# Rotary angles computed on 32 columns and spread through DRAM instead of on 512 columns in place

## Chip, cores and metric

One core of a Trainium2 chip runs the whole kernel. The metric is the device time of one execution in microseconds (us).

## What is computed

A two-layer decoder trunk on 512 tokens of width 1024: in each layer a token mixer (windowed attention with rotary positions, a gated delta rule, a causal convolution module) and a channel mixer. All matrix products are made of three products of split fp32 parts. What matters here is the rotary part: 8 frequencies, 512 positions, and the first 16 of every 64 head rows rotated.

```python
inv_freq = ROPE_THETA ** (-jnp.arange(0, ROT_DIM, 2, dtype=jnp.float32) / ROT_DIM)   # 8 values
ang = positions.astype(jnp.float32)[..., None] * inv_freq                              # 512 x 8
cos = jnp.cos(ang)[:, :, None, :]
sin = jnp.sin(ang)[:, :, None, :]
...
r1 = (x1 * cos - x2 * sin).astype(x.dtype)
r2 = (x2 * cos + x1 * sin).astype(x.dtype)
return jnp.concatenate([r1, r2, x[..., ROT_DIM:]], axis=-1)
```

## The kernel before

Activations lie feature-major: a tile holds 128 features on the partitions and 512 tokens as columns. Every engine has its own program, written out by hand, and the engines meet through semaphores; each engine does its instructions in order. A weight tile is loaded (`load_tile`, SyncE), its high part is written by ScalarE (`split`, L1293), the rest by VectorE (`split`, L1766), and TensorE makes 24 matmuls of 512 columns from it (`part`, L660). Two raw buffers alternate, so SyncE loads tile g when VectorE has split tile g - 2.

*Start.* SyncE issues, one after another, the parameters (L453), the positions broadcast to 128 partitions (L454), the last 9 columns of the constants (L455), the first constants (L456), x (L457), eight conditioning tiles of 1 MB (`load_ada`, L419), weight tiles 0 and 1 and the remaining constants. TensorE turns each conditioning tile into a row (L623), ScalarE copies it (L1347), TensorE sums it into columns (L631). When all eight are done, VectorE forms the modulation and `sclg`. ScalarE has split weight tiles 0 and 1 by then. Then, for each of 8 chunks k, ScalarE writes `hhi` (L1319), and VectorE the full value (L1861) and `hlo` (through the helper at L1756). TensorE bridges the wait with filler matmuls (`busy`, L687) and then does `first_pair` (L674 to L676): 48 matmuls, the two first weight tiles against the chunks as they come, and behind it the gates (L708 to L710).

*Angles.* On GpSimd, right behind a fill of `ZERO`: cast the positions, multiply by the frequency of the partition, then a range reduction for sine and cosine, 13 operations each (L561 to L571), with a semaphore wait behind every one (`turn`). All are on `ang`, 128x512, although only 32 of 128 rows carry an angle. ScalarE takes the sines in its step t = 2 (L1495, L1496), into `sinb` and `cosb`. VectorE masks the rows that are not rotated in its step t = 10 (L2046, L2047). Its `roped` (L1967) uses both five times in each layer, from step t = 13 on.

*Shared memory.* `posi` and `ang` lie in the room of conditioning tiles 8 and 9. So `load_ada(8)`, which SyncE comes to in its step t = 3 between weight tiles 5 and 6, waits on semaphore `sincos` (L414). Behind it on SyncE's list stand tile 9, weight tile 6 and a block of zeros for the DRAM array `xs`.

*Steps around it.* In step t = 4 ScalarE splits weight tile 6; at t = 5 it loads the table of logarithms and writes the logarithm of the key norms (`rows_logged`, L1389), then splits tile 7. TensorE uses that logarithm in `combine_rows` (L725, L726), behind tile 5 and ahead of tile 6.

Of the kernel before, what the change touches and what calls it, by code (L numbers as in the profile page):

```python
# [11 lines left out]
F32 = mybir.dt.float32  # L12
F32R = mybir.dt.float32r
I32 = mybir.dt.int32
# [4 lines left out]
P = 128  # L19
# [25 lines left out]
for _n, _w in (("ident", 128), ("ones", 128), ("pick", 1), ("eps", 1), ("pick8", 8), ("bones", 128), ("rot", 128), ("istk", 64), ("amask", 256),  # L45
               ("lev", 6 * 64), ("reset", 512), ("rows", 512), ("spread", 8 * 64), ("selg", 256),
               ("heads", 4 * 8), ("comb_r", 8), ("comb_l", 8), ("col_r", 16), ("col_l", 16), ("col_g", 16),
               ("i32", 32), ("half", 2), ("sign", 1), ("qscale", 1), ("rotm", 1), ("nrotm", 1), ("before", 128), ("blocks", 16), ("rank", 8), ("invf", 1)):
    C_COLS[_n] = (_at, _at + _w)
    _at += _w  # L50
N_CONST = _at
# [39 lines left out]
ORDER = [DK, DK + 1, DQ, DQ + 1, DV, DV + 1, CB, CB + 1, CA, CA + 1, V0, K0, Q0, Q0 + 1, Q0 + 2, Q0 + 3, DZ, DZ + 1]  # L91
I_CB, I_CA, I_V, I_K, I_Q, I_DZ = 6, 8, 10, 11, 12, 16
I_INV = 9


BY_PE = tuple(range(G_IN)) + (G_GATE, G_FFN - 1)
# [8 lines left out]
def constants():  # L105
    c = np.zeros((P, N_CONST), np.float32)

    def put(name, a):
        lo, hi = C_COLS[name]
        c[:a.shape[0], lo:hi] = a.reshape(a.shape[0], hi - lo)  # L110
# [58 lines left out]
    put("sign", np.where(p < 4, -1.0, 1.0)[:, None])  # L169
    put("qscale", np.where(p < 4, 0.0, -0.5 * np.log(64.0))[:, None])  # L170
    inv = np.float32(500000.0) ** (-np.arange(0, ROT, 2, dtype=np.float32) / np.float32(ROT))
    d = p % 64
    put("invf", np.where(d < ROT, inv[d % (ROT // 2)], 0.0)[:, None])
    put("rotm", (d < ROT)[:, None] * 1.0)
    put("nrotm", (d >= ROT)[:, None] * 1.0)
    put("eps", np.full((P, 1), EPS))
    put("rank", np.tile(8.0 - np.arange(8), (P, 1)))
    put("before", (p[:, None] < p[None, :]) * 1.0)
# [5 lines left out]
def trunk(nc, xT, consts, params, pos, ada, w8, w11, wm, outT):  # L184
    ctx = ExitStack()
    with ctx:
        def sb(name, shape, dt=F32, stack=ctx):
            return stack.enter_context(nc.sbuf_tensor(name, [P] + shape, dt))
# [3 lines left out]
        def sem(name):  # L192

            if name not in sems:
                sems[name] = ctx.enter_context(nc.semaphore(name))
            return sems[name]
# [24 lines left out]
            cact = sb("cact", [DC], stack=room)  # L221
        with ExitStack() as room:
            sb("below", [6 * KD * P + 13 * 1024], stack=room)
            posi = sb("posi", [S], I32, stack=room)
            ang = sb("ang", [5, S], stack=room)
        with ExitStack() as room:
            sb("above", [6 * KD * P + 25 * 1024 + 512], stack=room)
            wbah = sb("wbah", [DC * 8], F32R, stack=room)
# [28 lines left out]
            grow = sb("grow", [D], stack=room)  # L257
        xs = nc.dram_tensor("xs", (NB * P, D), F32, kind="Internal").ap()
        ys = nc.dram_tensor("ys", (NB * P, D), F32, kind="Internal").ap()

        def rawm_tile(g):
            return rawm[:, g % RING, :]
# [146 lines left out]
        def _(sp):  # L409

            def load_ada(g):

                if g == G_IN:
                    sp.wait_ge(sem("sincos"), 2)  # L414
                if g == G_GATE + 2:
                    sp.wait_ge(sem("ada_used"), G_GATE + 1)
                elif g >= G_IN + 2:
                    sp.wait_ge(sem("ada_acc"), summed(g - 2))
                sp.dma_start(adar(g), ada[g, :, :]).then_inc(sem(f"landed{ada_ring(g)}"), 16)  # L419
# [31 lines left out]
                sp.dma_start(out, src).then_inc(sem(f"tile_in{g % 2}"), 16)  # L451

            sp.dma_start(par[:], params).then_inc(sem("par_in"), 16)  # L453
            sp.dma_start(posi[:], pos.partition_broadcast(P)).then_inc(sem("pos_in"), 16)  # L454
            sp.dma_start(cst[:, N_CONST - 9:], consts[:, N_CONST - 9:]).then_inc(sem("pos_in"), 16)  # L455
            sp.dma_start(cst[:, 0:N_FIRST], consts[:, 0:N_FIRST]).then_inc(sem("cst_in"), 16)  # L456
            sp.dma_start(x[:], xT.rearrange("(c p) s -> p c s", p=P)).then_inc(sem("x_in"), 16)  # L457
# [5 lines left out]
            for t in range(N_IN_TILES):  # L463
                load_tile(t + 2)
                if t == 0:
                    sp.wait_ge(sem("zeroed"), 1)
                if t < NB:
                    sp.dma_start(xs[t * P:(t + 1) * P, :], ZERO).then_inc(sem("xs_cleared"), 16)
                if t == 3:
                    load_ada(G_IN)  # L470
                    load_ada(G_IN + 1)
                if t == 6:
                    load_ada(G_IN + 2)
                    load_ada(G_IN + 3)
# [62 lines left out]
        def _(pool):  # L537

            for name in ("bank_free0", "bank_free1", "glo_ready"):
                pool.sem_inc(sem(name), 1)  # L540
            pool.memset(ZERO, 0.0).then_inc(sem("zeroed"), 1)

            two_pi = 2 * np.pi
            c1 = 6.28125
            c2 = float(np.float32(np.round((two_pi - c1) * 2 ** 17) / 2 ** 17))
# [5 lines left out]
            def turn(ins):  # L551

                turned[0] += 1
                ins.then_inc(sem("ang_step"), 1)
                pool.wait_ge(sem("ang_step"), turned[0])

            pool.wait_ge(sem("pos_in"), 32)
            turn(pool.tensor_copy(ang[:, 0, :], posi[:]))
            turn(pool.tensor_scalar(ang[:, 0, :], ang[:, 0, :], C("invf"), None, ALU.mult))
            for n, shift in ((2, 0.0), (3, 0.25)):  # L560
                turn(pool.tensor_scalar(ang[:, 1, :], ang[:, 0, :], float(1 / two_pi), shift, ALU.mult, ALU.add))  # L561
                turn(pool.tensor_scalar(ang[:, 1, :], ang[:, 1, :], magic, None, ALU.add))
                turn(pool.tensor_scalar(ang[:, 1, :], ang[:, 1, :], magic, None, ALU.subtract))
                prev = ang[:, 0, :]
                for cc in (c1, c2, c3, c4):
                    turn(pool.tensor_scalar(ang[:, 4, :], ang[:, 1, :], -cc, None, ALU.mult))
                    turn(pool.tensor_tensor(ang[:, n, :], ang[:, 4, :], prev, ALU.add))
                    prev = ang[:, n, :]
                turn(pool.tensor_scalar(ang[:, n, :], ang[:, n, :], float(two_pi * shift), float(np.float32(3.1415925)),
                                        ALU.add, ALU.min))  # L570
                turn(pool.tensor_scalar(ang[:, n, :], ang[:, n, :], -float(np.float32(3.1415925)), None, ALU.max))  # L571

            pool.wait_ge(sem("xs_cleared"), 16 * NB)
            pool.wait_ge(sem("slots_ready"), 1)
# [702 lines left out]
        def _(act):  # L1277
# [86 lines left out]
            for layer in range(DEPTH):  # L1364
# [103 lines left out]
                for t in range(I_FILL):  # L1468
# [21 lines left out]
                    if t == 2:  # L1490
                        soft_plus()
                        gates()
                        if layer == 0:
                            act.wait_ge(sem("ang_step"), 2 + 2 * 13)
                            act.activation(sinb[:], ang[:, 2, :], ACT.Sin).then_inc(sem("sincos"), 1)  # L1495
                            act.activation(cosb[:], ang[:, 3, :], ACT.Sin).then_inc(sem("sincos"), 1)  # L1496
                    if t == 7:
                        queries_by_keys()
                    if t >= I_CB and not I_CA <= t < I_V:
# [240 lines left out]
        def _(dve):  # L1740
# [133 lines left out]
            for layer in range(DEPTH):  # L1874
# [92 lines left out]
                def roped(c):  # L1967

                    q = KT if c == 4 else QT[c]
                    at = 5 * layer + (1 if c == 4 else c + 2)  # L1970
                    dve.wait_ge(sem("rot_done"), at)
                    link(tt(ROTT, ps[:, 6, :], sinb[:]))
                    link(tt(q, q, cosb[:]))
                    mark(tt(q, q, ROTT, ALU.add), "roped")
# [45 lines left out]
                for t in range(I_FILL):  # L2020
# [20 lines left out]
                        decayed()  # L2041
                    if I_CA <= t < I_V:
                        gated_conv(t)
                    if t == 10 and layer == 0:
                        dve.wait_ge(sem("sincos"), 2)
                        link(dve.tensor_scalar(cosb[:], cosb[:], C("rotm"), C("nrotm"), ALU.mult, ALU.add))  # L2046
                        link(dve.tensor_scalar(sinb[:], sinb[:], C("rotm"), None, ALU.mult))  # L2047
                    if layer == 0 and t == 5:
                        ada_groups((G_IN,))
                        ada_groups((G_IN + 1,))  # L2050
# [361 lines left out]
```

## Time and profile before

| | |
|---|---|
| median of 3 runs | 1568.47 us (1567.01 to 1568.90) |
| profiled execution | 1568.9 us, span 1566.8 us |
| busy share TensorE / VectorE / ScalarE / GpSimd | 97% / 74% / 50% / 4% |
| mean granted TensorE clock | 0.98 |
| DMA | 340 MB, 217 GB/s mean |

The span goes from the first to the last instruction. A row of a timeline gives start and duration; operations of one engine overlap a little, so what an operation costs its engine is the distance to the next start. The granted clock is a share of 2.4 GHz: 1.00 or 0.50. A 512-column matmul starts every 0.23 us at full clock and every 0.43 us at half.

### The profile page before, as it was taken

The page shows a single profiled execution, that of the slowest core. Times are in us where ns is not written, and L with a number is a line of the kernel's source. Part 1 is how long each engine was busy: PE and PEld are TensorE (multiplying, and loading weights), DVE is VectorE, ACT ScalarE, POOL GpSimd, SP SyncE. Part 2 cuts the span into 40 slices and gives each one's busy share as a digit, 9 for nine tenths or more (in the row PEclk, how much of TensorE's full clock was granted, in tenths as well). Part 3 has the DMA queues.
Part 4 walks back from the last instruction along what each step waited for, and adds up shares of the span by engine and source line. Part 5 has one row for each costly group of instructions (what it writes and reads, how often), then busy time and mean ns, then how long its engine had stood idle before and what let it go on. Part 6 is the DMA issues. An engine that isn't in the chain of part 4 may idle for free.

```text
span 1566.8 us, 22640 instructions
## 1 busy us (share of the span) xinstructions
PE 1512.3 (97%) x9030; PEld 1205.6 (77%) x9030; DVE 1152.2 (74%) x1429; ACT 789.4 (50%) x937; POOL 64.1 (4%) x50
## 2 busy tenths in 40 slices
PE   5999999999999999999999999899999999999993
PEld 3668877778888888886688778688888888888883
DVE  4868866776666665446577764689999999999994
ACT  3534246332222222224543364677777777777774
POOL 8200000000000000000000000200000000000001
PEclk9989999999999999999999999999999999999996
DMA  9453212436655554531211005399999999999975
GB/s 358 141 203 109 82 41 69 169 129 198 188 185 185 182 189 153 180 109 54 68 55 44 27 28 190 110 414 410 400 399 399 399 391 396 391 396 399 399 274 174
DMA packets 94600, 340.30 MB, mean 217 GB/s; under 512 B 10016, under 2 KB 14240, under 8 KB 91808
## 3 DMA queue, kind: packets, MB, share of 16 engines
q1 hardware_dynamic: 92048, 329.95, 57.4%
q0 software_dynamic: 2448, 8.91, 1.5%
q8 instruction: 71, 1.16, 0.3%
q14 instruction: 33, 0.27, 0.1%
HBM read 316.81 MB, written 22.02 MB: 216 GB/s over the span
## 4 chain that ended last, share of the span: by engine, by line
PE 90%; DMA 4%; DVE 3%; issue 1%; ACT 1%; POOL 1%; SPq 0%; POOLq 0%; ACTq 0%; DVEq 0%
PE ps L660 36%; PE ps L1254 10%; PE ps L1252 10%; PE ps L1253 10%; PE ps L968 2%; DMA scr<-in_ada 2%; PE ps L996 1%; PE ps L823 1%; PE ps L816 1%; PE ps L980 1%; DMA xs<-sq,slots 1%; PE ps L612 1%; PE ps L1080 1%; PE ps L1082 1%; PE ps L1081 1%
## 5 line engine op out<-in xcount | busy, mean ns | idle before, releaser
L1756 DVE TENSOR_TENSOR wlm<-rawm,hlo 128x2048 fp32r<-128x2048 f32 x120 | 274.6, 2289 | 16.2 <-ACT hlo L1362 15.2
L1293 ACT ACTIVATE whi<-raw 128x1024 fp32r<-128x1024 f32 (+1 forms) x112 | 123.5, 1102 | 303.6 <-PE ps L660 254.4
L1362 ACT ACTIVATE hlo<-rawm 128x2048 fp32r<-128x2048 f32 x120 | 230.2, 1918 | 71.7 <-PE ps L1254 71.7
L660 PE MATMUL ps<-hhi,whi 128*128 128x512 f32 x624 | 253.3, 406 | 1.3 <-DVE wlo L1766 1.3
L1766 DVE TENSOR_TENSOR wlo<-raw,whi 128x1024 fp32r<-128x1024 f32 (+1 forms) x112 | 143.9, 1286 | 146.2 <-ACT whi L1293 144.1
L660 PE MATMUL ps<-hlo,whi 128*128 128x512 f32 x624 | 244.6, 392 | 0.0
L660 PE MATMUL ps<-hhi,wlo 128*128 128x512 f32 x624 | 244.5, 392 | 0.0
L1253 PE MATMUL ps<-wlm,xgh 128*128 128x512 f32 x480 | 186.7, 389 | 0.0
L1756 DVE TENSOR_TENSOR wlm<-rawm,whm 128x2048 fp32r<-128x2048 f32 x60 | 137.4, 2290 | 25.8 <-ACT whm L1362 25.8
L660 PEld LDWEIGHTS ps<-hhi,whi 128*128 128x128 f32 x624 | 117.9, 189 | 37.9 <-issue 12.7
L1252 PE MATMUL ps<-hlo,xgh 128*128 128x512 f32 x360 | 141.7, 394 | 1.5 <-ACT xgh L1678 1.5
L1254 PE MATMUL ps<-hlo,xgl 128*128 128x512 f32 x360 | 140.3, 390 | 0.0
L660 PEld LDWEIGHTS ps<-hhi,wlo 128*128 128x128 f32 x624 | 118.0, 189 | 26.0
L660 PEld LDWEIGHTS ps<-hlo,whi 128*128 128x128 f32 x624 | 118.1, 189 | 23.6 <-issue 1.0
L1362 ACT ACTIVATE whm<-rawm 128x2048 fp32r<-128x2048 f32 x60 | 114.9, 1916 | 17.2 <-PE ps L1254 17.2
L1253 PEld LDWEIGHTS ps<-wlm,xgh 128*128 128x128 f32 x480 | 90.2, 188 | 18.3
L1759 DVE SCALAR_TENSOR_TENSOR adas<-adah,cact,adas 128x256 f32<-128x256 f32 x196 | 94.9, 484 | 6.6
L1253 PE MATMUL ps<-wlm,hih 128*128 128x512 f32 x240 | 93.6, 390 | 0.0
L1759 DVE SCALAR_TENSOR_TENSOR scr<-scr,par 128x511 f32<-128x511 f32 (+26 forms) x120 | 82.8, 731 | 1.5
L1252 PEld LDWEIGHTS ps<-hlo,xgh 128*128 128x128 f32 x360 | 67.6, 188 | 15.1 <-ACT xgh L1678 1.6
L1254 PEld LDWEIGHTS ps<-hlo,xgl 128*128 128x128 f32 x360 | 67.6, 188 | 14.4
L660 PE MATMUL ps<-ghi,whi 128*128 128x512 f32 x176 | 69.3, 394 | 0.0
(332 smaller groups left out, 2528.8 us busy)
## 6 DMA issues: line engine op xcount, KB each, us to landing
rawm<-in_wm SPq DMA_DIRECT2D x360, 512.0 KB, 7.6
raw<-in_w SPq DMA_DIRECT2D x96, 512.0 KB, 3.6
adah<-in_ada SPq DMA_DIRECT2D x56, 512.0 KB, 4.3
scr<-in_ada SPq DMA_DIRECT2D x20, 1024.0 KB, 5.9
raw<-in_w SPq DMA_DIRECT2D x16, 704.0 KB, 4.1
xs<-scr SPq DMA_DIRECT2D x15, 512.0 KB, 5.3
ys<-yb SPq DMA_DIRECT2D x15, 512.0 KB, 8.4
xg<-xs SPq DMA_DIRECT2D x13, 512.0 KB, 7.1
```

The costliest lines, as they stand in the source:

```text
L612: ins = pe.matmul(ps[:, 7, 2 * g + m:2 * g + m + 1], ada_sum_in(g)[:, m * P:m * P + P], C("ones")[:, 0:1], start=True, stop=True)
L660: ins = pe.matmul(ps[:, b, :], a, r[:, k0 + k, :], start=(start and first and k == ks[0] and n == 0), stop=(stop and last and k == ks[-1] ...
L816: ins = pe.matmul(ps[cr, 2, u * 32:u * 32 + 32], cmp(MT)[cr, u, :], TCC[cr, u, :], start=True, stop=True)
L968: ins = pe.matmul(ps[:, b, c * 256 + lo:c * 256 + 256], QT[2 * b + c][r, n * P:(n + 1) * P], KT[r, (n - 1) * P + lo:(n + 1) * P], start=Tr ...
L1252: pe.matmul(ps[:, bank, :], ah[:, k, :], w_hi, start=(k == 0), stop=False)
L1253: pe.matmul(ps[:, bank, :], ah[:, k, :], w_lo, start=False, stop=False)
L1254: ins = pe.matmul(ps[:, bank, :], al[:, k, :], w_hi, start=False, stop=(k == DC - 1))
L1293: act.activation(whi[:, slot, 0:width], raw[:, slot, 0:width], ACT.Copy).then_inc(sem("hi_ready"), 1)
L1362: act.activation(hi_pair(q), raw_pair(q), ACT.Copy).then_inc(sem("him_ready"), 1)
L1756: return dve.tensor_tensor(out, a, b, op)
L1759: return dve.scalar_tensor_tensor(out=out, in0=a, scalar=s, in1=b, op0=op0, op1=op1)
L1766: dve.tensor_tensor(wlo[:, slot, 0:width], raw[:, slot, 0:width], whi[:, slot, 0:width].bitcast(F32), ALU.subtract).then_inc(sem("lo_ready ...
```

## The change

The angles are laid out as 8 frequencies by 16 blocks of 32 tokens: 128 partitions by 32 columns. Eight transfers bring the positions in this form, one for each frequency. GpSimd's chain is the same on 32 columns, and ahead of it GpSimd fills `cosb` with 1 and `sinb` with 0. ScalarE takes the sines in place. GpSimd waits for them, moves both to a DRAM scratch `trig`, waits for that, and issues eight transfers that lay the rows of 8 frequencies by 512 tokens into the rotated rows of `sinb` and `cosb`. SyncE's wait for `sincos` becomes one for the first of these transfers (`trig_moved` at 16). The masks on VectorE go, and each `roped` waits for all nine transfers.

```diff
+NF = ROT // 2
+POS_BLOCKS = P // NF
+POS_W = S // POS_BLOCKS
...
-    put("invf", np.where(d < ROT, inv[d % (ROT // 2)], 0.0)[:, None])
...
+    put("invf", inv[p // POS_BLOCKS][:, None])
...
-            posi = sb("posi", [S], I32, stack=room)
-            ang = sb("ang", [5, S], stack=room)
+            posi = sb("posi", [POS_W], I32, stack=room)
+            ang = sb("ang", [5, POS_W], stack=room)
...
+        trig = nc.dram_tensor("trig", (2, P, POS_W), F32, kind="Internal").ap()
...
                 if g == G_IN:
-                    sp.wait_ge(sem("sincos"), 2)
+                    sp.wait_ge(sem("trig_moved"), 16)
...
-            sp.dma_start(posi[:], pos.partition_broadcast(P)).then_inc(sem("pos_in"), 16)
+            for f in range(NF):
+                sp.dma_start(posi[f * POS_BLOCKS:(f + 1) * POS_BLOCKS, :], pos.rearrange("o (b j) -> (o b) j", j=POS_W))\
+                    .then_inc(sem("pos_in"), 16)
...
                 if t == 0:
-                    sp.wait_ge(sem("zeroed"), 1)
+                    sp.wait_ge(sem("ang_step"), 1)
...
-            pool.memset(ZERO, 0.0).then_inc(sem("zeroed"), 1)
-
...
-            pool.wait_ge(sem("pos_in"), 32)
+            turn(pool.memset(ZERO, 0.0))
+            turn(pool.memset(cosb[:], 1.0))
+            turn(pool.memset(sinb[:], 0.0))
+            pool.wait_ge(sem("pos_in"), 16 * (NF + 1))
...
+            pool.wait_ge(sem("sincos"), 2)
+            pool.dma_start(trig.rearrange("w p j -> p w j"), ang[:, 2:4, :]).then_inc(sem("trig_moved"), 16)
+            pool.wait_ge(sem("trig_moved"), 16)
+            for w, full in enumerate((sinb, cosb)):
+                for first in (0, NF, HD, HD + NF):
+                    pool.dma_start(full[first:first + NF, :], trig[w].rearrange("(f b) j -> f (b j)", f=NF))\
+                        .then_inc(sem("trig_moved"), 16)
...
-                            act.wait_ge(sem("ang_step"), 2 + 2 * 13)
-                            act.activation(sinb[:], ang[:, 2, :], ACT.Sin).then_inc(sem("sincos"), 1)
-                            act.activation(cosb[:], ang[:, 3, :], ACT.Sin).then_inc(sem("sincos"), 1)
+                            act.wait_ge(sem("ang_step"), 5 + 2 * 13)
+                            act.activation(ang[:, 2, :], ang[:, 2, :], ACT.Sin).then_inc(sem("sincos"), 1)
+                            act.activation(ang[:, 3, :], ang[:, 3, :], ACT.Sin).then_inc(sem("sincos"), 1)
...
+                    dve.wait_ge(sem("trig_moved"), 9 * 16)
                     dve.wait_ge(sem("rot_done"), at)
...
-                    if t == 10 and layer == 0:
-                        dve.wait_ge(sem("sincos"), 2)
-                        link(dve.tensor_scalar(cosb[:], cosb[:], C("rotm"), C("nrotm"), ALU.mult, ALU.add))
-                        link(dve.tensor_scalar(sinb[:], sinb[:], C("rotm"), None, ALU.mult))
```

## Rows read from the trace of the kernel before

**Rows 1.** The page's chain of waits, shares of the span by engine.

```profile
PE 90%; DMA 4%; DVE 3%; issue 1%; ACT 1%; POOL 1%; SPq 0%; POOLq 0%; ACTq 0%; DVEq 0%
```

**Rows 2.** The chain in order of time, 0 to 120 us: start, us, what.

```profile
7.73 24.77 DMA scr<-in_ada
...
63.90 5.67 PE ps L660 x24
```

**Rows 3.** Timeline of SyncE's queue: start, us, engine, line, out<-in, count.

```profile
1.20 0.42 SPq L454 DMA_DIRECT2D posi<-in_pos  x1
...
2.61 0.43 SPq L457 DMA_DIRECT2D x<-in_xT  x1
```

**Rows 4.** Timeline of TensorE, 26 to 56 us.

```profile
35.18 3.76 PE L687 MATMUL ps<-cst 128*128 128x256 f32 x8
40.82 0.76 PE L674 MATMUL ps<-hhi,whi 128*128 128x512 f32 x1 [1.88 <-DVE hlo L1756]
...
43.94 0.40 PE L675 MATMUL ps<-hlo,whi 128*128 128x512 f32 x1
...
54.53 0.39 PE L708 MATMUL ps<-hhi,wbah 128*8 128x512 f32 x1
```

**Rows 5.** Timeline of GpSimd: first and last of 28 angle operations.

```profile
5.03 0.61 POOL L558 CAST ang<-posi 128x512 f32<-128x512 int32 x1 [3.11 <-DMA cst<-in_consts]
...
47.39 1.54 POOL L571 TENSOR_SCALAR ang<-ang 128x512 f32<-128x512 f32 x1
```

**Rows 6.** Timeline of SyncE's queue around conditioning tile 8.

```profile
62.62 0.43 SPq L468 DMA_DIRECT2D xs<-scr  x1
73.10 0.80 SPq L419 DMA_DIRECT2D scr<-in_ada  x2
73.95 0.43 SPq L451 DMA_DIRECT2D raw<-in_w  x1
```

**Rows 7.** Timeline of ScalarE, 70 to 100 us.

```profile
72.46 0.61 ACT L1496 ACTIVATE cosb<-ang 128x512 f32<-128x512 f32 x1
...
83.78 1.06 ACT L1293 ACTIVATE whi<-raw 128x1024 fp32r<-128x1024 f32 x1 [5.84 <-DMA raw<-in_w]
...
86.15 0.68 ACT L1389 ACTIVATE scr<-ps,cst 8x512 f32<-8x512 f32 x1
...
96.54 0.21 ACT L1403 ACTIVATE small<-ps 128x48 f32<-128x48 f32 x1
```

**Rows 8.** Engines by microsecond: PE, PEld, DVE, ACT, POOL busy; clock, DMA, GB/s.

```profile
2.00:3.00 1.00, 0.00 (x0) 0.00 (x0) 0.00 (x0) 0.02 (x1) 0.00 (x0) 1.00 0.89 287
3.00:4.00 1.00, 0.00 (x0) 0.00 (x0) 0.00 (x0) 0.43 (x2) 0.00 (x0) 1.00 0.69 204
```

**Rows 9.** Timeline of VectorE, 35 to 58 us.

```profile
35.05 2.77 DVE L1766 TENSOR_TENSOR wlo<-raw,whi 128x1024 fp32r<-128x1024 f32 x2 [2.57 <-ACT whi L1293]
37.74 0.16 DVE L1756 TENSOR_TENSOR mod<-ps,par 128x16 f32<-128x16 f32 x1
37.94 1.05 DVE L1759 SCALAR_TENSOR_TENSOR sclg<-mod,par 128x8 f32<-128x8 f32 x1
39.03 0.92 DVE L1861 TENSOR_SCALAR scr<-scr,sclg,mod 128x512 f32<-128x512 f32 x1
...
49.85 0.54 DVE L1861 TENSOR_SCALAR scr<-scr,sclg,mod 128x512 f32<-128x512 f32 x1
...
51.04 0.54 DVE L1861 TENSOR_SCALAR scr<-scr,sclg,mod 128x512 f32<-128x512 f32 x1
...
56.60 1.23 DVE L1766 TENSOR_TENSOR wlo<-raw,whi 128x1024 fp32r<-128x1024 f32 x1
```

**Rows 10.** DMA issues: count, size, median us to landing; 0:160 and 1030:1050.

```profile
par<-in_params SPq DMA_DIRECT2D x1, 275.0 KB, 2.8
...
xg<-xs POOLq DMA_DIRECT2D x1, 512.0 KB, 7.0
```

**Rows 11.** Timeline of TensorE at the step that uses the logarithm.

```profile
87.75 1.02 PE L725 MATMUL ps<-scr,cst 8*8 8x512 f32 x2
```

**Rows 12.** Timeline of VectorE at step t = 10.

```profile
149.94 0.54 DVE L2046 TENSOR_SCALAR cosb<-cosb,cst 128x512 f32<-128x512 f32 x1
```

More of the change, by code:

```diff
@@ L47 @@
                ("heads", 4 * 8), ("comb_r", 8), ("comb_l", 8), ("col_r", 16), ("col_l", 16), ("col_g", 16),
-               ("i32", 32), ("half", 2), ("sign", 1), ("qscale", 1), ("rotm", 1), ("nrotm", 1), ("before", 128), ("blocks", 16), ("rank", 8), ("invf", 1)):
+               ("i32", 32), ("half", 2), ("sign", 1), ("qscale", 1), ("before", 128), ("blocks", 16), ("rank", 8), ("invf", 1)):
     C_COLS[_n] = (_at, _at + _w)
@@ L171, in constants @@
     inv = np.float32(500000.0) ** (-np.arange(0, ROT, 2, dtype=np.float32) / np.float32(ROT))
-    d = p % 64
-    put("invf", np.where(d < ROT, inv[d % (ROT // 2)], 0.0)[:, None])
-    put("rotm", (d < ROT)[:, None] * 1.0)
-    put("nrotm", (d >= ROT)[:, None] * 1.0)
+    put("invf", inv[p // POS_BLOCKS][:, None])
     put("eps", np.full((P, 1), EPS))
```

## The prediction, made before the change was built or timed

> **What bounds the kernel now.** I read the chain of waits first: nine tenths of it are TensorE [rows 1], so time can only move where that chain leaves TensorE or where TensorE runs at half clock. Everything the change touches lies in the first 160 us, so I went through that stretch engine by engine. The chain opens with DMA: the eight conditioning tiles land one behind the other until 32.50 us [rows 2], and their start is set by SyncE, which issues one transfer per 0.47 us, four transfers ahead of x at 2.61 [rows 3]. After the last tile comes a short relay (TensorE rows, ScalarE copy and weight split, VectorE), and at 40.82 us the first projection pair begins [rows 4]. From then to 109 us TensorE has no gap except the 0.3 us it waits for `hlo` chunks in the pair.
>
> Two other engines run beside this. GpSimd computes the angles from 5.03 to 48.93 us [rows 5], 28 operations on 128x512. VectorE's work in the relay overlaps the last 14 us of that. Further on SyncE stops for 10.0 us (63.05 to 73.10) before it loads conditioning tile 8, until the cosines are written [rows 6]; the weight tile that it issues behind it is used at 83.78 us by a ScalarE that sat idle for it [rows 7].
>
> **Part 1, the start of the loads.** The broadcast of positions, one transfer of 256 KB, becomes eight transfers of 2 KB. All eight stand on SyncE ahead of x and the conditioning tiles, so seven more issues come first: from 1.20 to 2.61 us three issues took 1.41 us, 0.47 us each [rows 3], and 7 x 0.47 = 3.3 us. Against that stands work that falls away: at 3 to 4 us the DMA engines were 0.69 busy [rows 8], so x's transfers had a small backlog before them; from 2 to 4 us they moved 491 KB, and parameters (275 KB), positions (256 KB) and constants (137 KB) ahead of x are some 0.68 MB: at most 0.2 MB, 0.5 us, was left at 4.0 us. The eight transfers cannot overlap x's issue. I take 3.3 - 0.5 = +2.7 us on the last landing (bounds: +2.1 if an issue of 16 short rows costs 0.33 us, like the weight tile at 73.95 [rows 6], and the backlog is kept out; +3.3 with no backlog). The whole relay hangs on that landing, so all of it is on the path.
>
> **Part 2, GpSimd leaves VectorE alone.** The angles shrink from 512 to 32 columns. An operation costs no more than the shortest on 512 columns, the cast with 0.61 us [rows 5]; even at that plus 0.1 between them, 28 end at about 8.5 + 20 = 28.5 us, before the relay (positions there at 8.5 by part 1). So no operation of GpSimd lies beside VectorE there. What that is worth: beside GpSimd six pairs (L1861, then the subtraction into `hlo`) took from 39.03 to 49.85, 1.80 us each; behind it one takes 51.04 - 49.85 = 1.19 us [rows 9]. The two weight subtractions took from 35.05 to 37.74 where a later one takes 1.23 us, some 1.15 from start to start: 0.3 us. The 8-column L1759 took 1.05 us [rows 9], right behind a 16-column addition of 0.16: 0.9 us. First pair: `hhi` of ScalarE is then what is awaited, so only 0.2 us. Sum ahead of the first matmul: -1.4 us.
>
> That the VectorE operation waits for GpSimd's is what the Trainium skill states as well (SBUF - State Buffer, the shared port pair: an exclusive lock held for a whole instruction). It names as losers VectorE operations in a two-port mode or with two SBUF inputs; L1861 has one tensor input, and the trace shows it slowed from 0.54 to 0.92 us all the same [rows 9]. By a strict reading only the subtractions would gain, about half of the pairs' difference; TensorE would still be the later of the two, so the sum stays.
>
> In the pair itself TensorE has 48 matmuls. Now: seven at half clock, 0.43 us each, until 43.94; then 41 until 54.53, 10.59 us, where 41 x 0.236 ([rows 2], 24 in 5.67 us) is 9.7: some 0.9 us of waits for `hlo` [rows 4]. With chunks every 1.19 us against 1.42 us of TensorE per chunk, TensorE is what is late next. It would start at 39.4 (times without part 1's shift), directly behind the filler matmuls, which end at 38.94. If the clock returns 3.1 us after the start, as now, the pair ends at 39.4 + 3.1 + 41 x 0.23 = 51.9 instead of 54.5: -2.6 us with the 1.4 in it. If the clock is back at once: 39.4 + 48 x 0.236 = 50.7, -3.8. If it stays at half until 47.5: 19 matmuls at half, 29 at full, 54.3, -0.2. The 0.7 us idle time that goes from before the pair speaks rather for an earlier return. I take -2.6. The Trainium skill (TensorE: Matmul & The Clock Gate, Part 1) says that the same program sees different numbers of slow matmuls from run to run; I leave that in the bounds.
>
> **Part 3, the later release of SyncE.** Now SyncE goes on at 73.07, with the second sine [rows 7]. Afterwards the two sines have 32 columns: 0.2 us each, like the 48-column exponential [rows 7], so they end at 72.3 instead of 73.07. Then GpSimd wakes, issues a transfer to DRAM of 256 pieces of 128 bytes, and SyncE waits for its landing. The trace has no such transfer. From below: the parameters, 275 KB from SyncE, land 2.8 us after the issue, of which 0.7 us is their size; so 2.1 us. From above: GpSimd's own transfer of 512 KB in full traffic, 7.0 us [rows 10]. DMA is empty at 73 us, so the lower row is nearer; I add half a microsecond for GpSimd's issue (0.58 us at L581): 2.7 us. SyncE goes on at 75.0, 1.9 us later than now (bounds 1.3 and 6.2). Behind the wait on SyncE stand conditioning tiles 8 and 9, weight tile 6 [rows 6] and a zero block of `xs`. Weight tile 6 thus reaches ScalarE 1.9 us after 83.78. In ScalarE's order a table load and the logarithm of the key norms follow; the logarithm ends at 86.83 [rows 7], and TensorE wants it at 87.75 [rows 11]. Slack 0.9 us: TensorE stalls for 1.9 - 0.9 = +1.0 us (bounds +0.4 and +5.3). Nothing gives it back: up to 104 us TensorE is gapless, and the next steps of the chain hang on its tile 6.
>
> In a sentence of its own: the Trainium skill (DMA: Bandwidth & Descriptors, the anatomy of a SWDGE transfer) gives about 2.0 us fixed plus bytes over 436 GB/s for a transfer issued from GpSimd; by that page, estimated, the stall would be 0.4 us instead of 1.0. No transfer of this trace shows it.
>
> **Part 4, what costs nothing.** The two mask operations of VectorE at 149.94, 1.1 us [rows 12], go; TensorE runs without a gap there, so 0 (at most -0.5 us). The sines give ScalarE 0.7 us at 72 us, behind which it waits for VectorE: 0. Three fills of GpSimd stand before 5 us, ahead of the positions: 0. The eight spreading transfers of 16 KB start at 75 us and are wanted at about 177 us: 0 for the rotation; on the engines they are 0.13 MB beside 2.6 MB, 0.3 us at most, in the bounds of part 3. Ten more semaphore waits on VectorE are already met: 0.
>
> **Sum.** +2.7 - 2.6 + 1.0 + 0 = +1.1 us on the profiled execution, 1568.9 us (span 1566.8 and 2.1 around it). The three runs of before have their median at 1568.47, 0.4 below that execution. I put the difference on the median: 1569.5.
>
> **Rivals.**
> *A, the transfer through DRAM is slow (ends slower).* Place: SyncE ahead of tile 8. If it lands in 7.0 us as in [rows 10], weight tile 6 is 6.2 us late and TensorE stalls 5.3: +2.7 - 2.6 + 5.3 = +5.4, 1573.9. It decides from a stall of 3.0 us, that is, a landing after 4.7 us. For it: 256 short pieces written to DRAM, and a queue that is not awake. Against it: an empty DMA at 73 us.
> *B, the clock does not help.* The pair stays at half clock: part 2 gives 0.2 only, +2.7 - 0.2 + 1.0 = +3.5, 1572.0. For it: the filler matmuls did not bring the clock back in 3.76 us. Against: it came back 3.1 us behind the pair's start.
> *C, the change doesn't clear GpSimd.* If an operation on 32 columns cost over 1.1 us, the angles would still lie beside the relay: part 2 falls away, +3.7, 1572.2. Against: a 512-column cast takes 0.61.
> *D, more gain than loss.* Short issues at 0.33 us, the clock back at once, the landing at its lower bound: +2.1 - 3.8 + 0.4 - 0.5 = -1.8, 1566.7. For faster by 0.2% it needs, on top, that the position transfers hardly delay x.
>
> **How the numbers follow.** About 0.2% (3.1 us) is what a measurement of this kernel can tell from no change. The forecast, with the rest of its bounds, 0.60; D within 0.2% adds 0.10, D beyond it 0.10; A 0.12; B and C together 0.08. So faster 0.10, same 0.70, slower 0.20. The range leaves out A's far end and D beyond 0.2%: from -3.0 to +5.5, 1565.5 to 1574.0.
>
> **What the profile would show.** Right: x issued near 5.9 us and the last conditioning tile 2 to 3 us later; GpSimd done before 25 us; the pairs at 1.2 us; the first pair about 12.5 us long; SyncE released 2 us behind the sines; a gap of about 1 us before L725's counterpart. Wrong: if x's landing hardly moves, part 1 falls; if VectorE's pairs stay over 1.4 us without GpSimd, the lock was not the cause; if the logarithm is in time, part 3 falls; and a clock fall at another place behind 88 us would move the time by microseconds that this sum does not have.

## The result, and the profile after

The changed kernel has a median of 1574.03 us over 20 runs, the kernel before 1569.03 over 20. One run of each took 3.8 ms; over the 19 others the medians are 1573.58 and 1568.90 us. The ratio, estimated from these, is 1.0029 with a 95% interval of 1.0018 to 1.0040: slower by 4.5 us (2.8 to 6.3), beyond the 3.1 us that a measurement of this kernel can tell from no change. The result stands at the upper end of the range, 1565.5 to 1574.0, and the forecast of +1.1 us was too low by 3.4 us. By the prediction's own line of 3.1 us the outcome is "slower", which had 0.20, and not "same", which had 0.70. The profiled execution took 1573.07 us, its span is 1571.2. From its page, the span and the busy shares:

```profile
span 1571.2 us, 22664 instructions
PE 1512.4 (96%) x9030; PEld 1206.7 (77%) x9030; DVE 1142.5 (73%) x1427; ACT 788.3 (50%) x937; POOL 37.8 (2%) x61
```

GpSimd has 26 us less to do and VectorE 10, but TensorE, which is busy for 96% of the time, does the same 9030 matmuls. So the places where TensorE starts are compared, as in the prediction. First SyncE's queue (timeline, start and duration), which answers [rows 3] and [rows 6]:

```profile
1.20 3.66 SPq L458 DMA_DIRECT2D posi<-in_pos  x8
...
5.84 0.43 SPq L462 DMA_DIRECT2D x<-in_xT  x1
...
63.29 0.43 SPq L473 DMA_DIRECT2D xs<-scr  x1
76.39 0.81 SPq L422 DMA_DIRECT2D scr<-in_ada  x2
77.24 0.43 SPq L454 DMA_DIRECT2D raw<-in_w  x1
```

Eight issues took 3.66 us, 0.46 each, although each moves 2 KB; x is issued 3.23 us later. SyncE stands idle from 63.72 to 76.39, 12.7 us instead of 10.0. TensorE, to [rows 4] and [rows 11]:

```profile
33.08 1.94 PE L637 MATMUL ps<-scr,cact 128*32 128x256 f32 x16 [2.12 <-DMA scr<-in_ada]
...
35.90 1.93 PE L637 MATMUL ps<-scr,cact 128*32 128x256 f32 x16
37.76 1.87 PE L645 MATMUL ps<-cst,scr 128*128 128x1 f32 x8
39.49 3.76 PE L701 MATMUL ps<-cst 128*128 128x256 f32 x8
43.69 0.77 PE L688 MATMUL ps<-hhi,whi 128*128 128x512 f32 x1 [0.45 <-DVE hlo L1770]
...
44.94 0.40 PE L688 MATMUL ps<-hhi,whi 128*128 128x512 f32 x1
...
55.18 0.39 PE L722 MATMUL ps<-hhi,wbah 128*8 128x512 f32 x1
...
90.12 1.01 PE L739 MATMUL ps<-scr,cst 8*8 8x512 f32 x2 [1.64 <-ACT scr L1403]
...
99.95 3.32 PE L764 MATMUL ps<-cst 128*64 128x256 f32 x16
...
106.15 1.12 PE L774 MATMUL ps<-scr,cst 8*128 8x512 f32 x2
```

The same two places in the kernel before:

```profile
96.22 3.68 PE L750 MATMUL ps<-cst 128*64 128x256 f32 x16
...
103.76 1.12 PE L760 MATMUL ps<-scr,cst 8*128 8x512 f32 x2
```

Three things are to be seen. The last conditioning tile is used 3.35 us later (35.90 against 32.55), and its 16 matmuls take 1.93 us, where the kernel before took 1.07: TensorE is at half clock here already. The pair itself is shorter, 11.5 us against 13.7, and ends only 0.65 us later. And behind tile 5 there is a new gap of 1.64 us at the logarithm. The pair's start adds up: 3.35 us for the later tile, 0.96 for the rows and sums at half clock (the fillers start at 39.49 instead of 35.18), less 1.43 because TensorE waits 0.45 us for `hlo` instead of 1.88, gives the 2.87 by which the pair starts later.

Which transfer holds up the start is shown by the chain of waits (start, us, what), here of the changed kernel:

```profile
9.64 23.40 DMA scr<-in_ada
33.08 1.94 PE ps L637 x16
```

It is the seventh conditioning tile, landing at 33.04, and not the eighth as in the kernel before [rows 2]: behind it TensorE does the seventh and the eighth without a gap, at half clock. VectorE, to [rows 9]:

```profile
41.73 0.17 DVE L1773 SCALAR_TENSOR_TENSOR sclg<-mod,par 128x8 f32<-128x8 f32 x1
...
43.46 0.54 DVE L1875 TENSOR_SCALAR scr<-scr,sclg,mod 128x512 f32<-128x512 f32 x1
...
50.57 0.54 DVE L1875 TENSOR_SCALAR scr<-scr,sclg,mod 128x512 f32<-128x512 f32 x1
```

Six pairs in 7.11 us, 1.19 each instead of 1.80, and 0.17 us for the 8-column operation that took 1.05. GpSimd's last angle operation and its transfer to DRAM, and ScalarE's second sine, its split of weight tile 6 and the logarithm (to [rows 5] and [rows 7]):

```profile
17.47 0.68 POOL L577 TENSOR_SCALAR ang<-ang 128x32 f32<-128x32 f32 x1
73.53 1.00 POOL L580 DMA_DIRECT2D trig<-ang  x1 [55.38 <-ACT ang L1510]
```

```profile
72.71 0.21 ACT L1510 ACTIVATE ang<-ang 128x32 f32<-128x32 f32 x1
...
86.92 1.06 ACT L1307 ACTIVATE whi<-raw 128x1024 fp32r<-128x1024 f32 x1 [8.34 <-DMA raw<-in_w]
...
89.30 0.68 ACT L1403 ACTIVATE scr<-ps,cst 8x512 f32<-8x512 f32 x1
```

From the end of the second sine (72.92, where 72.3 was forecast) to SyncE's next issue it is 3.5 us: 0.6 until GpSimd issues, 2.8 to the landing. Weight tile 6 comes to ScalarE 3.1 us later, its idle time grows from 5.84 to 8.34.

The clock behind the gap, from the view by stretches (columns as in [rows 8]), first the kernel before, then the changed one:

```profile
92.00:96.00 4.00, 4.00 (x31) 3.65 (x29) 3.75 (x9) 0.00 (x0) 0.00 (x0) 0.89 0.01 4
96.00:104.00 8.00, 8.00 (x31) 5.09 (x31) 6.16 (x11) 3.94 (x20) 0.00 (x0) 0.63 0.70 246
```

```profile
92.00:96.00 4.00, 4.00 (x11) 3.16 (x12) 3.68 (x7) 1.25 (x2) 0.00 (x0) 0.57 0.54 217
96.00:104.00 8.00, 8.00 (x50) 5.95 (x49) 7.38 (x13) 1.15 (x7) 0.00 (x0) 0.79 0.57 182
```

Both kernels have the same amount of half clock in these 12 us, a mean of 0.72. The kernel before loses the clock once, from 95.1 to 102.0 us. The changed kernel loses it twice, from 92.5 to 95.9, on matmuls of 512 columns, and from 99.3 to 102.8, where its 16 matmuls of L764 take 3.32 us. So between these two profiles the clock adds nothing here: TensorE is 2.37 us behind at the logarithm and 2.39 at the next place, 106.15 against 103.76. From 112.2 to 115.6 the kernel before loses the clock again and the changed one doesn't, so that the changed kernel is only 1.1 us behind from the values (124 us) to 250 us. The rest of the 4.4 us between the two spans comes in two half-clock stretches: at 273 us (3.4 us, none before) and at 331 us (10.2 us against 6.8).

### The profile page after: what moved, and what is told of

It is laid out like the page before. It is cut to its first block, busy times and chain, and to the rows that moved or that the text cites. A ratio compares the mean times of both kernels' runs of the same rounds, so it can differ in the third digit from the quotient of the medians.

```text
span 1571.2 us, 22664 instructions
## 1 busy us (share of the span) xinstructions
PE 1512.4 (96%) x9030; PEld 1206.7 (77%) x9030; DVE 1142.5 (73%) x1427; ACT 788.3 (50%) x937; POOL 37.8 (2%) x61
## 4 chain that ended last, share of the span: by engine, by line
PE 91%; DMA 3%; DVE 2%; ACT 2%; issue 1%; SPq 1%; POOL 0%; POOLq 0%; ACTq 0%; DVEq 0%
PE ps L674 34%; PE ps L1268 10%; PE ps L1266 10%; PE ps L1267 10%; PE ps L982 2%; DMA scr<-in_ada 1%; PE ps L1010 1%; PE ps L837 1%; PE ps L830 1%; PE ps L994 1%; PE ps L1094 1%; PE ps L626 1%; PE ps L1236 1%; PE ps L1095 1%; PE ps L1096 1%
## 5 line engine op out<-in xcount | busy, mean ns | idle before, releaser
L1267 PEld LDWEIGHTS ps<-wlm,xgh 128*128 128x128 f32 x480 | 90.2, 188 | 18.4
```

What stands on the lines that cost most here:

```text
L1267: pe.matmul(ps[:, bank, :], ah[:, k, :], w_lo, start=False, stop=False)
```

## The experiments

The table puts all profiles side by side: the start, in us from the first instruction, of the same matmul of TensorE in each. "Last tile" is the first matmul on the eighth conditioning tile, "pair" the first projection matmul, "behind it" the first gate matmul, "logarithm" the L725 of before, "query" the second L760, "values" the first L805. The ratio is to the kernel before on the same chip, with its 95% interval; it is estimated from all runs and is not the quotient of the two medians, from which it differs by up to 0.001. Microseconds given from a ratio are that share of 1569.

| kernel | last tile | pair | behind it | logarithm | query | values | ratio |
|---|---|---|---|---|---|---|---|
| before | 32.6 | 40.8 | 54.5 | 87.8 | 110.9 | 124.2 | |
| changed | 35.9 | 43.7 | 55.2 | 90.1 | 113.6 | 125.3 | 1.0029 (1.0018 to 1.0040) |
| again | 35.7 | 43.5 | 55.0 | 90.2 | 114.9 | 128.2 | 1.0020 (1.0005 to 1.0035) |
| late_start | 35.8 | 45.5 | 58.2 | 91.4 | 113.0 | 126.2 | 1.0025 (1.0011 to 1.0040) |
| late8 | 32.9 | 41.5 | 55.1 | 89.7 | 112.8 | 124.6 | 1.0025 (1.0007 to 1.0044) |
| late8_again | 33.0 | 41.3 | 55.0 | 89.5 | 112.7 | 124.4 | 1.0023 (1.0009 to 1.0037) |
| part2 | 32.8 | 40.5 | 52.2 | 85.5 | 107.3 | 119.0 | 0.9981 (0.9964 to 0.9999) |
| one_pos | 32.9 | 40.7 | 52.5 | 87.6 | 111.1 | 122.8 | 1.0008 (0.9991 to 1.0025) |
| own_room | 35.2 | 42.8 | 53.8 | 87.0 | 107.5 | 119.2 | 1.0001 (0.9986 to 1.0016) |
| tile_first | 35.2 | 43.0 | 54.5 | 87.7 | 110.9 | 124.2 | 0.9997 (0.9981 to 1.0013) |
| both | 33.0 | 40.8 | 51.8 | 85.0 | 105.5 | 117.2 | 0.9979 (0.9966 to 0.9992) |
| both_again | 32.5 | 40.3 | 51.8 | 85.0 | 106.9 | 118.6 | 0.9976 (0.9960 to 0.9992) |
| warm | 34.1 | 41.0 | 52.0 | 85.3 | 106.8 | 120.2 | 1.0002 (0.9983 to 1.0021) |
| beside | 36.1 | 44.6 | 57.5 | 93.0 | 119.4 | 132.7 | one execution, 1581.1 us |

My theory after the first profile: the three parts of the prediction are the whole effect, and two of them are larger than I priced them. The rival: the extra microseconds are the clock's, whose half-clock stretches lie elsewhere in each execution.

**The changed kernel again.** 

> The changed kernel once more, for a second profile. Theory of terms: its place in the first 120 us repeats: last conditioning tile +3.3 us, first pair ends +0.6, wait for the logarithm 1.6 us, and with half-clock matmuls behind that gap TensorE stands +2.5 to +4 us at 100 us. Rival, clock by chance: the half-clock stretches lie elsewhere in each profile, and of the +4.4 us of the first profile only what the first 120 us hold (about 1) comes back; the median then still lies 0.2 to 0.4% above before, because the mean over runs holds both.


The median was 1571.68 us. The first 90 us repeat within 0.2 us in the table; the wait at the logarithm is 1.9 us. From the query on the two profiles of one kernel differ by up to 3 us, and that is the clock: `again` is at half clock for 6.8 us from 99.3 on, where the first profile is for 3.4, and once more from 116.3 to 119.7. So the parts are real in each execution, and a single span can't weigh them: the rival explains the scatter, not the shift.

**Part 1 alone, in the kernel before.**

```diff
             sp.dma_start(posi[:], pos.partition_broadcast(P)).then_inc(sem("pos_in"), 16)
+            for f in range(7):
+                sp.dma_start(small[f * 16:(f + 1) * 16, 0:32].bitcast(I32), pos.rearrange("o (b j) -> (o b) j", j=32))\
+                    .then_inc(sem("pos_in"), 16)
...
-            pool.wait_ge(sem("pos_in"), 32)
+            pool.wait_ge(sem("pos_in"), 32 + 7 * 16)
```

> The kernel before with part 1 alone: seven more transfers of 2 KB on SyncE behind the positions. Theory: x is issued at 5.9, the last conditioning tile lands 3.0 to 3.3 us later and the first pair ends 3 us later, with GpSimd still beside VectorE. Rival (backlog hides the issues): 1 us or less. Rival (TensorE's clock falls earlier in the relay, as in the changed kernel): 4 us.


+0.25%, 3.9 us at before's 1569. The timeline of TensorE:

```profile
33.02 1.93 PE L626 MATMUL ps<-scr,cact 128*32 128x256 f32 x16 [1.78 <-DMA scr<-in_ada]
...
35.83 1.93 PE L626 MATMUL ps<-scr,cact 128*32 128x256 f32 x16
...
45.55 0.77 PE L677 MATMUL ps<-hhi,whi 128*128 128x512 f32 x1 [2.36 <-DVE hlo L1759]
```

The last tile is used 3.3 us later, and TensorE, which now waits 1.8 us for the seventh tile, does the relay at half clock: the pair starts 4.7 us later and ends 3.6 us later. The transfer itself is not that late. Its landing is seen where TensorE waits for the eighth tile, in `tile_first` (below):

```profile
10.02 25.18 DMA scr<-in_ada
```

It lands at 35.20, 2.7 us after the 32.50 of the kernel before [rows 2], and 0.5 us less than the 3.2 us of the issues: there the backlog came off as forecast. In `late_start` the eighth tile lands at 35.3, in the changed kernel at 35.6.

**Part 1 taken out of the change.**

```diff
-            for f in range(NF):
-                sp.dma_start(posi[f * POS_BLOCKS:(f + 1) * POS_BLOCKS, :], pos.rearrange("o (b j) -> (o b) j", j=POS_W))\
-                    .then_inc(sem("pos_in"), 16)
+            sp.dma_start(posi[:], pos.rearrange("o (b j) -> o b j", j=POS_W).broadcast_to([NF, POS_BLOCKS, POS_W]))\
+                .then_inc(sem("pos_in"), 16)
```

> The changed kernel with the eight position transfers made one (128 rows of 128 bytes, the blocks repeated by the source's pattern), so x is issued at 2.6 us again. Theory of terms: the last conditioning tile lands 3 us earlier, TensorE's first pair ends about 2 to 3 us before that of the kernel before, the stall behind tile 5 stays at 1.6 us: 3 us less than the changed kernel, about 1570.5 at the level of the first profiles. Rival, the queue's backlog hides the seven issues: no change against the changed kernel. Rival, clock only: no change either.


The median is 1569.86, and the ratio falls from the 1.0020 that the change had on this chip to 1.0008: 1.9 us less, 3.3 less than by its first ratio. The interval (0.9991 to 1.0025) holds 1.0020, so the ratio alone doesn't rule out the rivals. The place does: the pair ends 2.0 us before that of the kernel before and 2.6 us before that of the changed one; the wait at the logarithm stays at 1.8 us. What I missed:

```profile
1.20 0.78 SPq L457 DMA_DIRECT2D posi<-in_pos  x1
```

The issue of this one transfer takes 0.78 us instead of 0.42, so x is issued at 2.95 and not at 2.61. The last tile is used 0.4 us late, and the relay is still at half clock.

**Part 3 alone, in the kernel before.** GpSimd moves 32 columns of both angle rows to DRAM (their values are used by nobody), and SyncE waits for that.

```diff
                 if g == G_IN:
-                    sp.wait_ge(sem("sincos"), 2)
+                    sp.wait_ge(sem("xs_done"), 16)
...
+            pool.wait_ge(sem("sincos"), 2)
+            pool.dma_start(trig.rearrange("w p j -> p w j"), ang[:, 2:4, 0:32]).then_inc(sem("xs_done"), 16)
+            pool.wait_ge(sem("xs_done"), 16)
```

The three later waits on `xs_done` count 16 more.

> The kernel before with part 3 alone: GpSimd moves 32 columns of both sines to DRAM, and SyncE waits for that ahead of conditioning tile 8. Theory: SyncE goes on 3.4 us later, weight tile 6 arrives 3.3 us later, TensorE waits 2.2 to 2.5 us at the logarithm, and its clock falls behind that wait: +2 to +5 us at 100 us. Rival: the wait is given back at VectorE's wait at 110 us, +1 or less at 120 us.


+0.25%. GpSimd issues at 74.31 and SyncE goes on at 76.54, 2.9 us after the second sine's end at 73.69 and 3.4 us later than before, as expected; ScalarE gets weight tile 6 only 2.7 us later. The wait at the logarithm is shorter than the 2.2 to 2.5 us expected:

```profile
89.70 1.01 PE L730 MATMUL ps<-scr,cst 8*8 8x512 f32 x2 [1.26 <-ACT scr L1394]
...
93.13 0.63 PE L665 MATMUL ps<-hhi,whi 128*128 128x512 f32 x1
```

Behind it the clock falls at 92.9, and 512-column matmuls take 0.43 us from start to start. TensorE is 3.3 us behind at 96 us, but 1.9 at 106, as at the logarithm, because the stretch of the kernel before (95.1 to 102.0) is as long as the two of this one together. It is only 0.4 us behind at the values: in the profile of before a later half-clock stretch follows at 112 us that this one doesn't have. So the place gives both answers, and the median has to decide. The same kernel again, for the size of the part (the 1.9 us that the next expectation calls the wait are TensorE's lag at that place; the wait was 1.26):

> The kernel before with part 3 alone once more, for the size of that part and a second profile. Theory (the wait at the logarithm, 1.9 us in the first profile, plus half-clock matmuls behind it): ratio to before 1.0015 to 1.003, and half clock from about 92.5 us on instead of 95. Rival (only the stall less slack counts, as forecast): ratio 1.0003 to 1.001.


Again +0.23%, 3.6 us, with a wait of 1.2 us. The interval's lower end, 1.0009, rules out the rival (1.0003 to 1.001) but for its top; taken with the first run (lower end 1.0007) it is unlikely as a whole. What the part costs beyond the wait is not seen against the profile of before. The second is at half clock from 92.6 to 96.0 and from 99.4 to 102.8, together no longer than before's one stretch, and TensorE is 1.7 us behind at the logarithm, 1.7 behind it and 0.2 at the values. From 270 to 277 us both are at half clock, which costs 3.3 us, and the profile of before is not. But ten of the fourteen profiles have such a stretch there, `part2` and `both`, without any gap at the logarithm, among them, so the gap is not shown to be its cause. One profile of before is a poor yardstick for this; all fourteen together say more (see part 3 in the next section).

**The transfer through DRAM kept, its followers moved.**

```diff
-                if t == 3:
+                if t == 4:
                     load_ada(G_IN)
                     load_ada(G_IN + 1)
```

> The changed kernel with conditioning tiles 8 and 9 moved behind weight tile 6 on SyncE's list; the wait on the DRAM transfer stays. Theory (what is queued behind the wait makes the stall): weight tile 6 in time, no TensorE wait at the logarithm, like own_room, 3 us less than the changed kernel. Rival (traffic of the transfers through DRAM delays the tile): a wait of 1 us or more stays.


No wait at the logarithm, TensorE stands as in the kernel before from the gates to the values, ratio 0.9997: the cost of part 3 is neither the transfer nor its traffic but weight tile 6, which stood behind the wait on SyncE's list.

**The wait taken out.** Positions and angles lie in columns of `small` that are free until 96 us, so conditioning tile 8 waits for nothing.

```diff
+        posi = small[:, 0:POS_W].bitcast(I32)
+        ang = small[:, POS_W:6 * POS_W].rearrange("p (n j) -> p n j", n=5)
...
                 if g == G_IN:
-                    sp.wait_ge(sem("trig_moved"), 16)
```

> The changed kernel with positions and angles in columns of the small tile that are free then, so SyncE loads conditioning tile 8 without waiting for the transfer through DRAM. Theory of terms: weight tile 6 is in time, TensorE's 1.6 us wait goes and the half clock behind it moves or goes: 1.6 to 3.2 us less than the changed kernel. Rival, the tile-6 stall is only traded for a later wait (VectorE at 110 us): under 1 us less.


Ratio 1.0001, 3.0 us less than the changed kernel on this chip (1.0020), as the terms say, though the two intervals overlap. Its profile has a span of 1562.6, 4 us below what its median of 1568.82 would give: it has no half clock from 42 to 325 us. Whoever had judged by that span would have seen a gain of 4 us that the median doesn't have.

**Part 2 alone.** The two edits above, and SyncE waits for the sines as in the kernel before.

```diff
+                if g == G_IN:
+                    sp.wait_ge(sem("sincos"), 2)
```

> Part 2 alone: angles on 32 columns with one position transfer, in their own room, and SyncE waits ahead of conditioning tile 8 for the sines only, as in the kernel before; the way through DRAM is there but nobody on SyncE waits for it. Theory (the three parts add): first pair ends near 52 us (2.5 us before that of the kernel before), no wait at the logarithm, ratio to before 0.9975 to 0.999, since the changed kernel's +0.25% is +0.25 for the late start, +0.25 for the late tile and the rest. Rival (freed VectorE gives nothing to the end, the gain of `both` comes from SyncE's missing 10 us wait): ratio 0.9995 to 1.001.


Ratio 0.9981, 3.0 us less than before (0.2 to 5.6); the interval leaves the rival, 0.9995 to 1.001, a corner. The pair ends at 52.2, 2.3 us earlier, and nothing waits at the logarithm.

**GpSimd put beside VectorE again.**

```diff
+            for _ in range(20):
+                turn(pool.tensor_scalar(cosb[:], cosb[:], 1.0, None, ALU.mult))
             pool.wait_ge(sem("sincos"), 2)
```

> The changed kernel, with 20 multiplications by 1 of the 128x512 cosine tile on GpSimd behind the angles, so that GpSimd is beside VectorE from about 18 to 50 us again. Theory (the shared port prices part 2): the six-pair stretch of VectorE returns to 1.5 to 1.8 us a pair, the first pair of weight tiles ends 2.5 to 4 us later than in the changed kernel (58 to 59 us). Rival (VectorE was faster for another reason, the later start): it ends at 55 to 56 us.


VectorE's timeline, with GpSimd busy until 50.56, and behind that:

```profile
45.88 0.93 DVE L1877 TENSOR_SCALAR scr<-scr,sclg,mod 128x512 f32<-128x512 f32 x1
46.85 0.69 DVE L1772 TENSOR_TENSOR hlo<-scr,hhi 128x512 fp32r<-128x512 f32 x1
47.46 0.93 DVE L1877 TENSOR_SCALAR scr<-scr,sclg,mod 128x512 f32<-128x512 f32 x1
...
50.60 0.54 DVE L1877 TENSOR_SCALAR scr<-scr,sclg,mod 128x512 f32<-128x512 f32 x1
```

A pair takes 1.58 us beside GpSimd and 1.19 behind it; the first tile pair ends at 57.5, 2.4 us later than in the changed kernel. That is just below the 2.5 to 4 us expected and far from the rival's 55 to 56. This single execution took 1581.1 us, 8 us more than the profiled one of the changed kernel; some 5 us of that lie in half clock behind 92 us.

**Both edits, the fastest version.**

> Both edits together. Theory of terms: the terms add: 4.5 to 6 us less than the changed kernel, 0.5 to 2 us less than the kernel before (ratio 0.9987 to 0.9997 to it), since only the gain from GpSimd's absence is left. Rival, clock only: within 1 us of the changed kernel.


Ratio 0.9979: 3.3 us below the kernel before (the medians, 1567.55 and 1569.66 us, are 2.1 apart), and more than the 0.9987 to 0.9997 that the terms had given.

> The kernel `both` once more, to tell it from part2 and warm on one chip and to fix its ratio to the kernel before. Theory: 0.997 to 0.9985. Rival (the first ratio was luck of the clock): 0.999 to 1.0005.


Ratio 0.9976, 1565.18 us. Two intervals below 1 on two occasions: this version beats both kernels, by 0.2%. Against part2 it saves SyncE's wait for the sines, too, which gives no more than the intervals hide (0.9976 against 0.9981 on one chip).

**The relay kept at full clock.** Both edits, and fillers behind conditioning tiles 3 to 6.

```diff
                             condition_sum(g - 1)
+                        if 3 <= g < G_IN - 1:
+                            busy(7, 2)
```

> Both edits, and two filler matmul calls (256 columns, fp32) on TensorE behind each of conditioning tiles 3 to 6, in its waits for the loads. Theory (TensorE's short waits for the loads let its clock fall ahead of the relay, which costs the relay about 0.9 us and the pair 1 to 2): no half clock between 29 and 43 us, relay and pair 1.5 to 3 us shorter than in `both`. Rival (the fall comes from the low row count of the conditioning matmuls, fillers don't change it, or they only delay the last tile): first pair ends at 51.8 us or later.


The rival's case. TensorE, the eighth tile and the relay:

```profile
33.05 1.11 PE L696 MATMUL ps<-cst 128*128 128x256 f32 x4
34.09 1.07 PE L632 MATMUL ps<-scr,cact 128*32 128x256 f32 x16
35.09 1.18 PE L640 MATMUL ps<-cst,scr 128*128 128x1 f32 x8
36.13 1.97 PE L696 MATMUL ps<-cst 128*128 128x256 f32 x8
41.03 0.47 PE L683 MATMUL ps<-hhi,whi 128*128 128x512 f32 x1 [2.92 <-DVE hlo L1767]
```

The clock holds: 1.07 us for the rows of a tile, 1.97 for the fillers that took 3.76. But the fillers put the last tile's matmuls 1.1 us back (34.09 against 32.98), and the pair starts at 41.03 and ends at 52.0, behind the 40.78 and 51.8 of `both`. The ratio is 1.0002 (0.9983 to 1.0021), where `both_again` had 0.9976 on the same chip. At the start the half clock of the relay costs about what its cure costs; where the rest of these 4 us comes from, the first 60 us don't show, and this stays open.

## Why the prediction was right, and where it was low

*Bound and places: right.* Every place where the time went was named: x's issue, the last tile, the pairs, SyncE's release, the gap at L725. The three parts, each run alone, give +0.25%, +0.25% (and +0.23%) and -0.19%, together +0.3%, 4.7 us; the whole change measures +0.29%, 4.5 us. No fourth part is needed, but the three intervals together leave the sum open by about 4 us to either side, so a small one is not ruled out either.

*Part 1, +2.7 forecast: +3.9 measured, the landing right, the way behind it mis-sized.* The seven issues cost 3.23 us (3.3 said), and the last tile lands 2.7 us later where it can be seen (`tile_first`), as forecast; in the changed kernel it is 3.1. The step that failed is the next one, "the whole relay hangs on that landing, so all of it is on the path". The chain goes through the seventh tile: it lands at 33.04 instead of 29.3, TensorE, no longer behind the loads, waits about 2 us for it, is at half clock, and comes to the last tile 3.35 us later. The rows of that tile take 1.93 us instead of 1.07, and the relay loses another 1 us, a term that the sum did not have. So the pair ends 0.65 us later in the changed kernel, where the terms gave 0.1.

*Part 2, -2.6 forecast: -3.0 measured.* The pairs went to 1.19 us as taken, the 8-column operation to 0.17. The pair of weight tiles took 11.5 us against 12.5: the clock came back after three matmuls instead of seven, so the step "as now, 3.1 us after the start" was on the careful side. In `part2` it ended 2.3 us early, in `both` 2.7. The interval of the -3.0 goes from -0.2 to -5.6, so the places carry this part more than the time does. Rival B, the pair at half clock, did not come; rival C neither, GpSimd was done at 18.2.

`beside`, in which only GpSimd's work was added, brings the slow pairs back, so it is GpSimd that slows VectorE. The Trainium skill (SBUF - State Buffer, Who interferes with whom) says that one of the two engines waits for the whole of the other's instruction; that they slow each other agrees, that it is for a whole instruction no run here shows. As losers it names VectorE operations with two SBUF inputs or in a two-port mode, and it lists `tensor_scalar` among those that can be in one. L1877, which has one tensor input, went from 0.54 to 0.93 us; no trace here shows its mode.

*Part 3, +1.0 forecast: +3.6 to +3.9 measured. This is the term that was mis-sized most.* The step "2.7 us from sine to SyncE" measured 3.5 us in the changed kernel, 2.9 in `late8`, and the second sine ended 0.6 us later than taken. I had counted GpSimd's issue with 0.58 us; it took 1.00, and 0.6 us pass before it. The slack of 0.9 was right: the delay of weight tile 6 relative to TensorE, 3.1 - 0.65 = 2.5 us, less 0.9, is 1.6, and TensorE waited 1.64. That accounts for 0.6 us of the miss. Rival A, a landing later than 4.7 us, did not come, though the end that it forecast, slower, did.

The larger rest, some 2 us, is that I priced the gap as a gap. "A clock fall at another place behind 88 us" stands in the prediction as what the sum does not have, and the fall did move: in all five profiles of the changed kernel, `one_pos` and `late8` the clock is at half 2.3 to 3.2 us behind the logarithm's start, on projection matmuls, where the kernel before loses it at 95, on small ones. Against the one profile of before it costs nothing: in four of the five TensorE's lag at the next place, 106 us in the changed kernel, is that at the logarithm. Against all profiles it does. From the logarithm to the values TensorE took 34.9 to 39.7 us in the six profiles with the gap (mean 36.3) and 32.2 to 36.5 in the eight without it (mean 34.3): 2 us more, all in half clock, since the granted clock of that stretch is 0.78 to 0.90 in the six and 0.86 to 1.00 in the eight. The two groups overlap, and before's own profile is among the slowest of the eight, so this makes the clock the likely cause and doesn't prove it. What the ratios show is that without the gap the cost is gone: `tile_first` and `own_room` have none, and theirs are 0.9997 and 1.0001.

From GpSimd's issue to the landing the trace has 2.8 us, for 32 KB in 256 pieces. The Trainium skill (DMA: Bandwidth & Descriptors, Anatomy of one DMA) gives a fixed cost of some 2.0 us for a transfer that GpSimd issues, by which, estimated, the stall would have been 0.4 us. The measurement differs and decides: the stall was 1.64.

*The rest, 0: right.* VectorE's masks, the sines and the spreading transfers moved nothing: the last of the eight was issued at 80 us, and `tile_first`, which has all of them, stands at the values where before stands.

*Luck.* That the first profile is 1.1 us behind from 124 to 250 us, the very number forecast, is chance: `again` is 4.0 behind there. And in the sum 0.4 us too little gain in part 2 stood against 3.8 too little cost in the two others.

*What stays open.* The 2 us of part 3 beyond the gap rest on groups of profiles that overlap, and not on a comparison of two. The 19 runs of the changed kernel go from 1568.28 us at a mean clock of 0.983 to 1582.22 at 0.975; 0.008 of 1571 us are 12.6 us, most of the 13.9 between them. Why a stretch falls near 270 us in some executions and not in others was not settled.

## What to carry to other kernels

What a transfer costs the engine that issues it hardly depends on its size (0.46 us for 2 KB, 0.47 for 256 KB): ahead of the loads that bound the start, eight transfers of 2 KB hold up everything behind them by 3.7 us, so fold them into one access pattern (0.78 us). When a wait on a queue is moved to a later event, price what is queued behind it, and put the urgent transfer ahead of the wait. When loads come later, look at each of them and not only at the last: here the seventh set the pace. And judge by medians: a profile's span carries several microseconds of where the half-clock stretches happened to fall. A gap on TensorE can cost more than its length in half clock behind it. But to say so, add up the half clock of both kernels over the whole place, and in several profiles of each: a stretch that comes earlier may only replace another.

## What the runs showed of the hardware that I had not expected

Delaying the loads can slow TensorE: in eight profiles in which it waits 1.4 us or more for the seventh conditioning tile, the clock fell at 28 to 32 us instead of 33.7, and the last tile's 16 matmuls took 1.93 us instead of 1.07. The wait alone doesn't fix the moment: `tile_first` waits 1.9 us and `own_room` 1.4, too, and their clock fell at 33.8 and 35.5. With fillers in the waits (`warm`) it did not fall. A transfer issued by GpSimd begins 0.6 us after the semaphore that it waits for, and its issue takes 1.00 us for 256 pieces, against 0.5 us for the eight that follow it.
